# Seven block products instead of eight for one K group of the down projection, in a two-layer encoder trunk on Trainium2

## What is computed

```python
D_FF = 5632
a, b = jnp.split(rms_norm(x, norm_ffn) @ w_gate_up, 2, axis=-1)   # 256 x 5632 each
return x + (jax.nn.silu(a) * b) @ w_down                          # w_down: 5632 x 2048
```

## Time and profile before

| | |
|---|---|
| runs (us) | 2724.33, 2724.59, 2724.8 |
| span of the profiled execution (us) | 2722.7 |
| PE busy | 2716.4 us, 100% |
| PEld busy | 2251.5 us, 83% |
| DVE busy | 1903.3 us, 70% |
| ACT busy | 1261.4 us, 46% |
| POOL busy | 119.6 us, 4% |
| mean rate of all DMA | 196 GB/s |
| granted TensorE clock | 1.000 |

### The profile page before, as it was taken

How to read it: one execution, slowest core, us unless ns; L and a number is a source line. 1 busy time by engine, 2 the same in 40 slices (tenths; PEclk the granted TensorE clock), 3 DMA queues, 4 the chain that set the end, 5 groups by cost and what they waited for, 6 DMA issues and landing times.

```text
span 2722.7 us, 30019 instructions
## 1 busy us (share of the span) xinstructions
PE 2716.4 (100%) x12090; PEld 2251.5 (83%) x12090; DVE 1903.3 (70%) x2515; ACT 1261.4 (46%) x1511; POOL 119.6 (4%) x90
## 2 busy tenths in 40 slices
PE   9999999999999999999999999999999999999999
PEld 7888888888888888888888888888888888888887
DVE  7888566688766576556878885666887665775665
ACT  6555444444444344434454654444454443444443
POOL 0001000122000000000000010001210000000000
PEclk9999999999999999999999999999999999999999
DMA  9554555555555555555555545555555555555553
GB/s 367 193 194 154 188 202 197 201 186 215 185 201 196 191 196 221 197 190 198 189 185 186 195 152 186 203 205 194 185 201 190 197 195 191 196 190 197 184 204 141
DMA packets 77802, 533.76 MB, mean 196 GB/s; under 512 B 8896, under 2 KB 9152, under 8 KB 15072
## 3 DMA queue, kind: packets, MB, share of 16 engines
q1 hardware_dynamic: 74800, 523.67, 53.5%
q0 software_dynamic: 2288, 7.47, 1.0%
q10 hardware_dynamic: 576, 0.71, 0.1%
HBM read 529.72 MB, written 2.10 MB: 195 GB/s over the span
## 4 chain that ended last, share of the span: by engine, by line
PE 97%; DVE 1%; DVEq 0%; ACT 0%; DMA 0%; POOL 0%; issue 0%; ACTq 0%
PE acc L354 32%; PE acc L355 32%; PE acc L353 32%; PE acc L421 1%; DVE w_lo L862 0%; PE tr L433 0%; PE tr L450 0%; PE tr L449 0%; PE tr L451 0%; ACT rows L626 0%; DMA y<-memT_in 0%; ACT w_hi L581 0%; POOL prob_b L295 0%; DVEq L1031 0%; PE acc L483 0%
## 5 line engine op out<-in xcount | busy, mean ns | idle before, releaser
L862 DVE TENSOR_TENSOR w_lo<-raw,w_hi 128x1024 fp32r<-128x1024 f32 x945 | 1162.7, 1235 | 764.0 <-ACT w_hi L581 754.8
L581 ACT ACTIVATE w_hi<-raw 128x1024 fp32r<-128x1024 f32 x975 | 1030.5, 1061 | 1345.1 <-PE acc L355 1341.6
L353 PE MATMUL acc<-w_hi,b_hi 128*128 128x512 f32 x1952 | 761.1, 390 | 0.7 <-DVE b_lo L1081 0.7
L354 PE MATMUL acc<-w_lo,b_hi 128*128 128x512 f32 x1952 | 760.2, 389 | 0.0
L355 PE MATMUL acc<-w_hi,b_lo 128*128 128x512 f32 x1952 | 759.9, 389 | 0.0
L353 PE MATMUL acc<-w_hi,a_hi 128*128 128x512 f32 x1944 | 757.3, 390 | 0.0
L354 PE MATMUL acc<-w_lo,a_hi 128*128 128x512 f32 x1944 | 756.4, 389 | 0.0
L355 PE MATMUL acc<-w_hi,a_lo 128*128 128x512 f32 x1944 | 756.3, 389 | 0.0
L353 PEld LDWEIGHTS acc<-w_hi,b_hi 128*128 128x128 f32 x1952 | 366.9, 188 | 77.5 <-issue 1.4
L355 PEld LDWEIGHTS acc<-w_hi,b_lo 128*128 128x128 f32 x1952 | 366.8, 188 | 76.1
L354 PEld LDWEIGHTS acc<-w_lo,b_hi 128*128 128x128 f32 x1952 | 366.9, 188 | 75.9
(11 more groups left out here) (148 smaller groups left out, 834.5 us busy)
## 6 DMA issues: line engine op xcount, KB each, us to landing
raw<-weights SPq DMA_DIRECT2D x484, 1024.0 KB, 4.8
bias<-bias_in POOLq DMA_DIRECT2D x24, 256.0 KB, 4.5
raw<-weights SPq DMA_DIRECT2D x7, 512.0 KB, 9.1
y<-memT_in SPq DMA_DIRECT2D x14, 256.0 KB, 6.6
rows<-mem_in SPq DMA_DIRECT2D x1, 2048.0 KB, 16.3
x<-xT_in SPq DMA_DIRECT2D x1, 2048.0 KB, 20.7
x<-x_in SPq DMA_DIRECT2D x1, 2048.0 KB, 7.3
out<-x SPq DMA_DIRECT2D x3, 512.0 KB, 7.5
```

The source lines that it names most:

```text
L353: pe.matmul(o, hi[:, kt + k, tok], wh, start=first and k == 0, stop=False)
L354: pe.matmul(o, hi[:, kt + k, tok], wl, start=False, stop=False)
L581: act.activation(w_hi[:, h % SPLIT_SLOTS, :], raw[:, slot, part * HALF:(part + 1) * HALF], ACT.Copy).then_inc(hi_ready, 1)
L862: dve.tensor_tensor(w_lo[:, h % SPLIT_SLOTS, :], raw[:, slot, part * HALF:(part + 1) * HALF], w_hi[:, h % SPLIT_SLOTS, :].bitcast(F32), AL ...
```

## The change

Column chunks of the down projection go in pairs (0 with 1, 2 with 3), in the two full parts of each layer. Of the four K groups (4 K blocks each) of a pair, groups 1 to 3 are computed as before. Group 0 is seen as a 2x2 matrix of blocks times a 2x2 matrix of blocks: A (2 token blocks by 2 halves of K) times B (2 halves of K by 2 column chunks). Eight block products would do it, each with one half of weights and one token block, which is 6 matmuls. The change takes seven, by the scheme of Strassen in Winograd's form. The sums of A's blocks are made once per part (`seven_operands`), split in `s_hi` and `s_lo`; the sums of B's blocks are made by DVE in place in `raw`, four times 128x1024, between the splits (`split_seven`); the seven products go to seven PSUM places, among them the two banks of `tr` and the spare accumulator, and DVE puts them together with small additions before it adds to x (`down_pair`). Since each product has its own weight operand, group 0 has 7 splits on ACT and on DVE in place of 4. The stream of units is put in the order of `PAIR_ORDER`, three units (6 halves) ahead of group 0. Some tiles (`mem_v`, `turn`) move into unused parts of `y`; `a_raw`, `s_raw` and the sums lie in `mem_qT` and `mem_kT`.

```diff
+PAIR_ORDER = ((0, 1), (0, 2), (1, 1), (0, 0), (1, 0), (0, 3), (1, 2), (1, 3))
...
+            def split_seven():                                  # ACT
+                r = n.at("raw")
+                wait_raw(r)
+                wait_raw(r + 2)
+                for i, part in enumerate((0, 1, 3, 3, 2, 0, 1)):
+                    h = n.at("half")
+                    act.wait_ge(half_used, h - SPLIT_SLOTS + 1)
+                    if i >= 3:
+                        n.add("t")
+                        act.wait_ge(t_ready, n.at("t"))
+                    act.activation(w_hi[:, h % SPLIT_SLOTS, :], raw_half(r + part), ACT.Copy).then_inc(hi_ready, 1)
+                    n.add("half")
+                n.add("raw", 4)
+                act.wait_ge(half_used, n.at("half", 1 - SEVEN))
+                act.activation(upper_sums[:, 0, :], tr_banks[:, 0, :], ACT.Copy).then_inc(first_copied, 1)
...
+                        if j == j0 and groups == PART:          # ACT
+                            act.activation(a_raw, tr[:, :, :], ACT.Copy).then_inc(a_copied, 1)
+                            n.add("s")
+                            act.wait_ge(s_sums, n.at("s"))
+                            act.activation(s_hi[:, :, :, :], s_raw, ACT.Copy).then_inc(s_hi_ready, 1)
...
+            def split_seven():                                  # DVE
+                r = n.at("raw")
+                b11, b21, b12, b22 = [raw_half(r + i) for i in range(4)]
+                for i, part in enumerate((0, 1, 3, 3, 2, 0, 1)):
+                    dve.wait_ge(hi_ready, n.at("half", 1))
+                    low_part(r + part)
+                    n.add("half")
+                    if i == 2:
+                        dve.tensor_tensor(b22, b22, b12, ALU.subtract).then_inc(t_ready, 1)
+                        dve.tensor_tensor(b12, b12, b11, ALU.subtract).then_inc(t_ready, 1)
+                        dve.drain()
+                        dve.tensor_tensor(b11, b22, b11, ALU.add).then_inc(t_ready, 1)
+                    if i == 3:
+                        dve.drain()
+                        dve.tensor_tensor(b21, b21, b11, ALU.subtract).then_inc(t_ready, 1)
+                n.add("raw", 4)
...
+                def seven_operands():                           # DVE
+                    a11, a12 = a_raw[:, 0:HALF_KT, 0:P], a_raw[:, HALF_KT:, 0:P]
+                    a21, a22 = a_raw[:, 0:HALF_KT, P:], a_raw[:, HALF_KT:, P:]
+                    dve.wait_ge(a_copied, n.at("s", 1))
+                    dve.tensor_tensor(s_raw[:, 0, :, :], a21, a22, ALU.add)
+                    dve.tensor_tensor(s_raw[:, 2, :, :], a11, a21, ALU.subtract)
+                    dve.drain()
+                    dve.tensor_tensor(s_raw[:, 1, :, :], s_raw[:, 0, :, :], a11, ALU.subtract)
+                    dve.drain()
+                    dve.tensor_tensor(s_raw[:, 3, :, :], a12, s_raw[:, 1, :, :], ALU.subtract).then_inc(s_sums, 1)
+
+                def seven_operands_lo():
+                    n.add("s")
+                    dve.wait_ge(s_hi_ready, n.at("s"))
+                    dve.tensor_tensor(s_lo[:, :, :, :], s_raw, s_hi[:, :, :, :].bitcast(F32), ALU.subtract
+                                      ).then_inc(s_ready, 1)
...
+                        if j == j0 and groups == PART:
+                            seven_operands()
                         op_plain(kts(j - j0))
+                        if j == j0 and groups == PART:
+                            seven_operands_lo()
...
-                        chunk(acc_of[0], *B, need={0: 1, 6: 0})
-                        for c in range(1, NC):
-                            chunk(acc_of[c], *B)
+                        pe.wait_ge(tr_free, n.at("tr"))
+                        for c in range(0, NC, 2):
+                            left, right = acc_of[c], acc_of[c + 1]
+                            group(left, *B, 1, first=True)
+                            group(left, *B, 2)
+                            group(right, *B, 1, first=True)
+                            seven_products(left, right, 3 - left - right, *B)
+                            group(left, *B, 3, last=True)
+                            group(right, *B, 2)
+                            group(right, *B, 3, last=True)
```

More of the change, by code:

```diff
@@ L78, in layer_stream @@
                 order.append(a[j + 1])
-        if j0 + n < ACT_GROUPS:
-            order += [(w_down[j0 * COLS:(j0 + n) * COLS], c) for c in range(NC)]
+        if n == PART:
+            for c0 in range(0, NC, 2):
+                order += [(w_down[(j0 + g) * COLS:(j0 + g + 1) * COLS], c0 + c) for c, g in PAIR_ORDER]
         else:
@@ L141, in trunk @@
         rows = sb("rows", [P, 6, TB, COLS])
-        mem_v = sb("mem_v", [P, TB, COLS])
+        s_hi = sb("s_hi", [P, 4, HALF_KT, P], F32R)
+        s_lo = sb("s_lo", [P, 4, HALF_KT, P], F32R)
         mem_kT = sb("mem_kT", [P, N_MEM, SEQ])
@@ L377, in last_pair, with group, product, seven_products @@
                 n.add("half", 2)
+            def group(acc_i, hi, lo, g, first=False, last=False):
+                if first:
+                    pe.wait_ge(taken[acc_i], n.at(f"acc{acc_i}", 1))
+                    n.add(f"acc{acc_i}")
+                half(acc_i, hi, lo, 4 * g, first, False)
+                half(acc_i, hi, lo, 4 * g + HALF_KT, False, last)
+            def product(o, hi, lo, first=False):
+                at = n.at("half")
+                slot = at % SPLIT_SLOTS
+                pe.wait_ge(lo_ready, at + 1 - pool_before(at + 1))
+                for k in range(HALF_KT):
+                    wh, wl = w_hi[:, slot, columns(k)], w_lo[:, slot, columns(k)]
+                    pe.matmul(o, hi[:, k, :], wh, start=first and k == 0, stop=False)
+                    pe.matmul(o, hi[:, k, :], wl, start=False, stop=False)
+                    mm = pe.matmul(o, lo[:, k, :], wh, start=False, stop=first and k == HALF_KT - 1)
+                mm.then_inc(half_used, 1)
+                n.add("half")
+            def seven_products(left, right, spare, hi, lo):
+                pe.wait_ge(taken[spare], n.at(f"acc{spare}", 1))
+                n.add(f"acc{spare}")
+                pe.wait_ge(tr_free, n.at("tr", 1))
+                n.add("tr")
+                n.add("seven")
+                pe.wait_ge(s_ready, (n.at("seven") + 1) // 2)
+                upper, lower = slice(0, HALF_KT), slice(HALF_KT, 2 * HALF_KT)
+                t0, t1 = slice(0, P), slice(P, 2 * P)
+                product(tr_banks[:, 0, :], hi[:, upper, t0], lo[:, upper, t0], True)
+                product(acc[left][:, 0, :], hi[:, lower, t0], lo[:, lower, t0])
+                product(acc[right][:, 0, :], s_hi[:, 3, :, :], s_lo[:, 3, :, :])
+                product(tr_banks[:, 1, :], s_hi[:, 2, :, :], s_lo[:, 2, :, :], True)
+                product(acc[spare][:, 1, :], s_hi[:, 0, :, :], s_lo[:, 0, :, :], True)
+                product(acc[spare][:, 0, :], s_hi[:, 1, :, :], s_lo[:, 1, :, :], True)
+                product(acc[left][:, 1, :], hi[:, lower, t1], lo[:, lower, t1])
             def chunk(acc_i, hi, lo, halves=FULL, kt=0, first=0, upto=None, need=()):
```

114 lines of the change are left out of this document (88 added, 26 removed).

## The result

The changed kernel takes 2731.67 us (median of 9 runs, 2731.36 to 2731.88), the kernel before 2724.49 us in the same comparison. The ratio is 1.0026, with a 95% interval of 1.0017 to 1.0036: it is slower, by 7.2 us. The profiled execution has a span of 2729.9 us for 2722.7 before.

The account below looks back on a forecast made before the run. PE was taken to bound the kernel, busy 2716.4 of 2722.7 us. The terms -10.9 + 14.3 + 3.8 = +7.2 us took the median from 2724.6 to 2731.8 us, range 2724 to 2735.5.

Parts of the forecast that it names:

- The saving: Down projection, group 0 of each pair on PE: 48 matmuls fewer at 0.2267 us, 10.9 us less.
- The pairs: Group 0 of each pair: DVE's sums and splits make product 5 1.79 us late, eight times, 14.3 us more.
- chain of seven steps: DVE at a pair, third split to end of product 5's split: 855.99 to 864.43, 8.44 us.
- The first operand: First operand of each full part: sums of A's blocks delay a split, PE 0.94 us late, four times, 3.8 us more.
- What was costed at nothing: Down projection loads and PE's new waits, and the tiles moved into `y`: no added time.
- DVE's chain doesn't decide: Rival at the pairs: product 5's split done before 862.64, PE runs through; 2717.5 or 2713.7 us; chance 0.06.
- The stops are smaller than the saving: Rival at pairs and first operands: PE resumes at once, drains cost little, no measurable change; 2726 to 2730 us; chance 0.27.
- The stops cost more than their length: Rival on PE: each of twelve stops throws the clock back for about nine matmuls; 22 us, 2753 us; chance 0.03.
- the 2734.7 us: Time if, by the skill page's rule, four steps of the pair's DVE chain took 1.22 us or more, not 1.14.
- the idle time of PE: Sign in the profile after: some 18 us put down to DVE, before 4th and 5th products and at first operands.

Follow-up runs that it names:

- the kernel with both rearrangements: Changed kernel with A's block sums moved to the next group, the B22 product first and the weight-block sums spread between splits: 2713.59 us, ratio 0.9960.
- the added instruction: Changed kernel with one more 128x1024 DVE instruction ahead of the first sum of weight blocks in each seven: 2740.87 us, ratio 1.0061.

## Why the prediction was right

2731.8 us was forecast and 2731.67 measured; the span was forecast at 2729.9 and is 2729.9. The experiments tell whether the terms were right one by one, or only their sum. They were right one by one, to within half a microsecond. That the sum came out to a tenth is luck: the cost of the pairs was forecast some 0.5 us too high, and 0.3 us came from outside the pairs and the first operands (at the end of this section).

- **The saving**, forecast 10.9 us: the kernel with both rearrangements is 10.9 us faster than before and has the same matmuls as the changed one. Right. On PE the matmuls of the products stand 0.2267 us apart, as those of plain halves do.
- **The pairs**, forecast 14.3 us: 14.15 us went when the sums were spread (1.77 per use). In the trace of the changed kernel a use takes 11.24 to 11.28 us for 9.52, which makes 13.8 us in eight. Right, by the mechanism told. The chain of seven steps starts where it was said to: forecast 855.99 to 864.43, which is 8.44 us; measured 857.05 to 865.46, 8.41 us. It all lies about 1 us later since the stop at the first operand came before. The sums in `raw` take 1.22 us, as taken from the earlier trace rows.
- **The first operand**, forecast 3.8 us: 4.2 us by moving it, 3.9 us by adding it alone to eight products. Right. DVE's chain there, with A = 704.11 for the start of ACT's operand copy, was forecast to start its first sum at A + 2.00, `s_lo` at A + 4.93 and the next split at A + 6.07:

```profile
706.08 0.42 DVE L1504 TENSOR_TENSOR mem_kT<-mem_qT 128x256 f32<-128x256 f32 x1 [0.75 <-ACT mem_qT L925]
...
708.97 1.23 DVE L1514 TENSOR_TENSOR s_lo<-mem_kT,s_hi 128x1024 fp32r<-128x1024 f32 x1
710.11 4.62 DVE L968 TENSOR_TENSOR w_lo<-raw,w_hi 128x1024 fp32r<-128x1024 f32 x4
...
711.48 0.47 PE L383 MATMUL acc<-w_hi,a_hi 128*128 128x512 f32 x1 [0.69 <-DVE w_lo L968]
```

  They stand at A + 1.97, A + 4.86 and A + 6.00. The last row is PE's, the stop itself.
- **What was costed at nothing** (order of units, moved tiles, PE's new waits, loads): eight products in the new order measure as the kernel before, within 0.1%. That run doesn't show PE's waits for the spare accumulator and for `s_ready`, nor the two slots of `raw` that stay occupied through a use of the scheme. In the changed kernel DMA moves 12 GB/s in that stretch (the second row of busy times above); in the kernel before it moves 181 at the same place, as this row of its busy times shows:

```profile
857.40:866.90 9.50, 9.50 (x44) 7.86 (x43) 4.84 (x5) 4.24 (x4) 0.00 (x0) 1.00 0.56 181
```

  Yet PE's list of waits has none for a load, and ACT waits for weights only in the first 45 us, in both kernels alike (1.98 us the longest). The kernel with both rearrangements, which has the same waits of PE and holds the slots as well, loses nothing.
- **The rivals.** "DVE's chain doesn't decide" is out by the added instruction (9.2 us). "The stops are smaller than the saving" is out; its cheap drains and cheap restarts aren't there: a sum behind a drain starts 0.09 us after the end of the last one (859.33 + 1.22 = 860.55 to 860.64). "The stops cost more than their length" is out: there were twenty stops (the prediction reckoned this rival with twelve), the matmuls behind each stand 0.23 us apart again, for 0.43 at the start of the program, and the granted clock is 1.00. The prediction gives only half of what the Trainium skill says on the page "VectorE: DVE Perf Modes", section "The DRAIN you can't avoid". By that half each step would have been as long as its instruction or longer. The same paragraph adds: "A next op that is not held starts earlier". With that the trace agrees: steps without a drain are 1.14 us for instructions of 1.22 to 1.23 us. So the page taken whole doesn't ask for the 2734.7 us.
- **What was off:** the idle time of PE. Some 18 us put down to DVE were expected; the waits list 11.9 us (6.4 + 2.8 + 2.7). It is a matter of reading, not of time. The record of a matmul is 0.39 us long where its successor may start after 0.23, and the record of the first after a stop begins 0.11 us early and is 0.50 long: the next one starts 0.34 after it (863.05 to 863.39) for 0.23 otherwise. Each stop at a product thus shows 0.16 + 0.11 = 0.27 us less idle time than it costs. At the four plain halves the first record is 0.47 us long and the next starts 0.30 after it (711.48 to 711.78), which makes 0.24. Together that is 5.3 us, and 11.9 + 5.3 = 17.2. The forecast delays sum to 18.1 us.

What is left is small, and the two traces settle most of it. Both hold every matmul (12090 and 12042), so each can be compared with the one of the same place in the order. PE was 0.42 us later than before already at its first matmul of a plain half (7.79 for 7.37), where it waited longer for the operand that comes from memory; but from the 50th matmul on 0.15 us of it is left, and it is the same just before the first stop, here in the kernel before and in the changed one:

```profile
707.76 0.39 PE L353 MATMUL acc<-w_hi,a_hi 128*128 128x512 f32 x1
...
707.91 0.39 PE L383 MATMUL acc<-w_hi,a_hi 128*128 128x512 f32 x1
```

From there each of the eight uses adds 0.36 to 0.40 us (2.97 in all), each of the four first operands 0.95 to 0.97 (3.86), and 0.17 comes between the last use of layer 0 and the first operand of layer 1. The sum is 0.15 + 2.97 + 3.86 + 0.17 = 7.15 us, and the last matmul of the program starts 7.15 us later than before. What makes the 0.15 and the 0.17 stays open. Such differences are no larger than what the runs scatter.

## What to carry to other kernels

In this kernel the ring of four slots gives the engines ahead of PE a lead that can't be saved up: DVE idles 1.50 us right before the chain with which it makes PE late. What counts is not how busy DVE is over a stage, but the longest chain that it must run between the moment at which PE frees a slot and the moment at which PE wants its content. Before a product is removed from PE, write that chain down with its start, and compare its end with the due time, which moves nearer when products get shorter. And put preparatory work where DVE waits for PE's slots anyway, one instruction per gap: the same four sums cost 14 us behind one another and nothing spread out.

## What the runs showed of the hardware

- DVE's instructions of 128x1024 float32 on tiles in SBUF, in place on their own source too, start 1.14 us apart and take 1.22 us; with a drain between, the next starts 0.09 us after the end. All eight chains of the changed kernel are 8.40 us long, to within 0.01. The exceptions are the three named above, one in each run with an added instruction, with 0.35 us more behind a drain.
- PE resumes at once after a stop of 0.3 to 1.5 us. At the products the weight load starts 0.05 us after the split's end (864.23 + 1.23 = 865.46):

```profile
865.50 0.19 PEld L422 LDWEIGHTS acc<-w_hi,s_hi 128*128 128x128 f32 x1 [1.23 <-DVE w_lo L968]
```

  At the four first operands it starts 0.11 us after it; the runs don't tell why. The matmuls behind a stop come only about 0.01 us farther apart than usual, and the granted clock didn't change.
- Idle time of PE that is put down to a releaser understates a stop by 0.24 to 0.27 us here; with many short stops that is a third of the loss.
